# Merging the last gate products, the out-projection and the MLP of a transformer layer into one block

## The reference, cut to what matters

```python
    g_f, g_d, g_g, g_c = jnp.split(jax.nn.sigmoid(gate_logits), N_BRANCHES, axis=-1)
    merged = (g_f * (y_f @ lp['w_br_fourier']) + g_d * (o_d @ lp['w_br_diff'])
              + g_g * (o_g @ lp['w_br_gqa']) + g_c * (y_c @ lp['w_br_conv']))
    return merged @ lp['w_out']
...
# then, per stream, with rms norms and modulation:
x = x + gx1 * rms_norm(mixer_out); x = x + gx2 * rms_norm(sq_relu_mlp(modulate(x)))
```

## Time and profile before

| | us |
|---|---|
| median of 3 runs | 3958.98 |
| lowest, highest run | 3958.79, 3963.68 |
| span of the profiled execution (first to last instruction) | 3959.9 |
| PE busy in it | 3646.2 (92%) |
| DVE, ACT, POOL busy in it | 1911.9, 1398.4, 131.7 |
| mean granted PE clock, share of full speed | 0.953 |

### The profile page before, as it was taken

The page is one execution under the profiler, slowest core; times in us unless marked ns, Lnnn a source line. Parts: engine busy times, 40 slices in busy tenths (PEclk is TensorE's granted clock), DMA queues, the critical chain, the costliest instruction groups (busy, mean ns, idle before and its releaser), DMA issues. The chain is left out here.

```text
span 3959.9 us, 47862 instructions
## 1 busy us (share of the span) xinstructions
PE 3646.2 (92%) x18756; PEld 2836.1 (72%) x18756; DVE 1911.9 (48%) x2912; ACT 1398.4 (35%) x2388; POOL 131.7 (3%) x90
## 2 busy tenths in 40 slices
PE   6989898979999999998897999989998999989999
PEld 2878897855677778884773567778887776677767
DVE  0756565655544354441475654434443346433553
ACT  2454433224443322222423444332222435334342
POOL 0000000010000010001001000010001000000000
PEclk9999898999999989997998999989998999989999
DMA  8425453320112323326331112223332221222212
GB/s 312 149 91 155 123 165 129 100 70 28 47 60 69 107 64 93 94 91 266 123 92 36 43 49 64 85 71 95 96 96 87 67 65 51 70 89 66 60 45 94
DMA packets 97407, 371.75 MB, mean 94 GB/s; under 512 B 11184, under 2 KB 11440, under 8 KB 95280
## 3 DMA queue, kind: packets, MB, share of 16 engines
q1 hardware_dynamic: 97200, 368.82, 29.2%
HBM read 357.25 MB, written 11.53 MB: 93 GB/s over the span
## 5 line engine op out<-in xcount | busy, mean ns | idle before, releaser
L368 DVE TENSOR_TENSOR w_lo<-w_raw,w_hi 128x1024 fp32r<-128x1024 f32 x527 | 644.9, 1224 | 776.7 <-ACT w_hi L358 776.4
L382 PE MATMUL banks<-h_hi,w_hi 128*128 128x512 f32 (+2 forms) x2040 | 790.3, 387 | 28.2 <-DVE h_lo L1005 9.8
L384 PE MATMUL banks<-h_hi,w_lo 128*128 128x512 f32 (+2 forms) x2040 | 749.5, 367 | 0.0
L383 PE MATMUL banks<-h_lo,w_hi 128*128 128x512 f32 (+2 forms) x2040 | 749.3, 367 | 0.0
L358 ACT ACTIVATE w_hi<-w_raw 128x1024 fp32r<-128x1024 f32 x545 | 573.0, 1053 | 363.6 <-DMA w_raw<-in_stream 361.6
L382 PEld LDWEIGHTS banks<-h_hi,w_hi 128*128 128x128 f32 (+1 forms) x2040 | 391.1, 192 | 118.6 <-issue 35.5
L384 PEld LDWEIGHTS banks<-h_hi,w_lo 128*128 128x128 f32 (+1 forms) x2040 | 390.1, 191 | 66.4
L383 PEld LDWEIGHTS banks<-h_lo,w_hi 128*128 128x128 f32 (+1 forms) x2040 | 391.9, 192 | 56.6 <-issue 3.8
L382 PE MATMUL banks<-merged_hi,w_hi 128*128 128x512 f32 (+1 forms) x960 | 350.0, 365 | 28.1 <-PEq L2320 10.7
L384 PE MATMUL banks<-merged_hi,w_lo 128*128 128x512 f32 (+1 forms) x960 | 346.4, 361 | 0.0
L383 PE MATMUL banks<-merged_lo,w_hi 128*128 128x512 f32 (+1 forms) x960 | 345.6, 360 | 0.0
(11 more groups left out here) (322 smaller groups left out, 4988.6 us busy)
## 6 DMA issues: line engine op xcount, KB each, us to landing
w_raw<-in_stream SPq DMA_DIRECT2D x593, 512.0 KB, 3.6
w_whole<-in_stream SPq DMA_DIRECT2D x48, 512.0 KB, 8.9
x_kept<-x SPq DMA_DIRECT2D x4, 2048.0 KB, 7.2
x<-x_kept SPq DMA_DIRECT2D x4, 2048.0 KB, 8.1
dft_table<-in_dft SPq DMA_DIRECT2D x2, 2048.0 KB, 8.1
x<-in_x SPq DMA_DIRECT2D x1, 2048.0 KB, 11.2
out_x<-x SPq DMA_DIRECT2D x8, 256.0 KB, 4.4
late_consts<-in_consts SPq DMA_DIRECT2D x1, 1152.0 KB, 5.5
```

Source lines behind the costliest of these rows:

```text
L368: (by or self.nc.vector).tensor_tensor(self.lo[:, c], self.raw[:, c], self.hi[:, c].bitcast(F32), ALU.subtract)\
L382: self.nc.tensor.matmul(out, w_hi, x_hi, start=start, stop=False)
L383: self.nc.tensor.matmul(out, w_hi, x_lo, start=False, stop=False)
L384: mm = self.nc.tensor.matmul(out, w_lo, x_hi, start=False, stop=stop)
```

## The change

The function `merge_last_branch` goes. Its PE, ACT and DVE parts stand at the head of the parts of `rest_stage`, in the same block as the out-projection. PE's first out-projection tile waits, ahead of each k, for `merged_lo[k]`. The block of `begin_transfer` for `x` goes too: SP issues that DMA as its first instruction of the joined block, so ahead of the last gate products instead of behind them, and ahead of the weight loads of that block. POOL and DVE wait for it before the first residual, as they did. As the two blocks' buffers now live together, `y` is laid over `branch_sum`, `mid_hi` and `mid_lo` over `h`, the squares over the gate tiles; `x` is placed from the top of memory (`take_high`), and the three little tiles of the norm that outlives the function have fixed homes. No arithmetic is added or removed.

```diff
@@ -435,6 +435,19 @@
         self.held.append((at, at + size, t.name))
         return t
 
+    def take_high(self, name, shape, dt=F32):
+        size = -(-4 * int(np.prod(shape)) // 64) * 64
+        at = self.high - size
+        for a, b, _ in sorted(self.held, key=lambda h: -h[0]):
+            if b <= at:
+                break
+            at = min(at, a - size)
+        assert at >= self.low, (name, size)
+        self.n += 1
+        t = self.nc.alloc_sbuf_tensor_at(f"{name}_{self.n}", [P] + list(shape), dt, offset=at)
+        self.held.append((at, at + size, t.name))
+        return t
+
     def over(self, name, t, dt, shape=None, skip=0):
 
         self.n += 1
@@ -881,12 +894,13 @@
 
 
 
-    def __init__(self, K, name, n_tiles, NT, at, rows_bank):
+    def __init__(self, K, name, n_tiles, NT, at, rows_bank, home=None):
         self.K, self.n, self.NT, self.nt = K, n_tiles, NT, NT // P
         self.sums = K.ps[:, 7, at:at + n_tiles * self.nt]
         self.rows = K.ps[:, rows_bank, 0:NT]
         self.sq = None
-        self.mean, self.rt, self.rstd = (K.take(f"{name}_{t}", [self.nt]) for t in ("mean", "root", "rstd"))
+        self.own = [K.take(f"{name}_{t}", [self.nt]) for t in ("mean", "root", "rstd")] if home is None else []
+        self.mean, self.rt, self.rstd = [t[:] for t in self.own] or [home[:, j] for j in range(3)]
         S = lambda t: K.count_of(f"{name}_{t}")
         self.squared, self.summed, self.averaged = S("squared"), S("summed"), S("averaged")
         self.rooted, self.inverse, self.turned = S("rooted"), S("inverse"), S("turned")
...
@@ -1011,7 +1025,7 @@
             s.advance(self.n)
 
 
-def rest_stage(K, x, merged, mod, mods, NT, following):
+def rest_stage(K, x, merged, mod, mods, NT, following, gates, h, kept):
@@ -1022,15 +1036,16 @@
     scaled, added = S("rest_scaled"), (S("rest_added_dve"), S("rest_added_pool"))
     up_free, down_free, mid_hi_ready, mid_lo_ready = S("mlp_up_bank_free"), S("mlp_down_bank_free"), S("mlp_mid_hi"), S("mlp_mid_lo")
     h_hi, h_lo = merged
-    c0, up, turns = W.used, W.used + KD, FF_T // 8
-    per = 2 * CHUNK
-    x_in = [(count.sem, count.at(value)) for count, value, _ in K.owed]
+    gates.merged = merged
+    c0, turns = gates.ends.next_block // CHUNK, FF_T // 8
+    up, per = c0 + KD, 2 * CHUNK
+    x_in = K.count_of("x_in")
     with ExitStack() as scope, K.block() as block:
-        y = K.sb(scope, "y", [KD, NT])
-        mid_hi = K.sb(scope, "mid_hi", [8, NT], F32R)
-        mid_lo = K.sb(scope, "mid_lo", [8, NT], F32R)
+        y = K.over("y", gates.acc, F32)
+        mid_hi = K.over("mid_hi", h[0], F32R)
+        mid_lo = K.over("mid_lo", h[1], F32R)
         m = K.sb(scope, "mid", [2, NT])
-        sq = K.sb(scope, "squares", [4, NT])
+        sq = K.over("squares", gates.sg, F32)
         table = K.sb(scope, "table_load", [1])
         post_mix = RowNorm(K, "post_mix", KD, NT, 0, 4)
         pre_mlp = RowNorm(K, "pre_mlp", KD, NT, 32, 5)
@@ -1040,18 +1055,31 @@
                 norm.sq = sq
         lead = Lead(K, pre_mlp, x, mods[:, 2], mod[:, 24:32], h_hi, h_lo, NT, False)
         lead.t = m
+
+        @block.sync
+        def _(sp):
+            if kept is not None:
+                sp.dma_start(x[:].rearrange("p k n -> p (k n)"), kept).then_inc(x_in.sem, 16)
         run_pipeline_ahead(K, block, up + per * turns)
         K.settle(block)
 
+        def wait_x(eng):
+            if kept is not None:
+                eng.wait_ge(x_in.sem, x_in.at(16))
+
         def wait_added(eng, n):
             eng.wait_ge(added[n % 2].sem, added[n % 2].at(n // 2 + 1))
 
         @block.tensor
         def _(pe):
+            for _ in gates.pe(pe, 2):
+                pass
             for f in range(KD):
                 if f >= 4:
                     pe.wait_ge(post_mix.squared.sem, post_mix.squared.at(f - 3))
                 for k in range(KD):
+                    if f == 0:
+                        pe.wait_ge(gates.out_lo.sem, gates.out_lo.at(k + 1))
                     W.multiply(pe, K.ps[:, f % 4, 0:NT], (c0 + f) * CHUNK + k, h_hi[:, k, 0:NT], h_lo[:, k, 0:NT],
                                k == 0, k == KD - 1)
                 if f >= 1:
@@ -1092,6 +1120,8 @@
 
         @block.scalar
         def _(act):
+            for _ in gates.act(act, 2):
+                pass
             nc.scalar.activation(table[:], K.eps[:], ACT.Sqrt)
             for f in range(KD):
                 W.split_hi(act, c0 + f + AHEAD)
@@ -1130,8 +1160,7 @@
                     nc.gpsimd.tensor_tensor(x[:, f, 0:NT], x[:, f, 0:NT], m[:, f % 2], ALU.add).then_inc(added[1].sem, 1)
 
             lead.pool(pool, range(up + AHEAD, up + SLOTS))
-            for sem, value in x_in:
-                pool.wait_ge(sem, value)
+            wait_x(pool)
             residual(0)
             residual(KD)
@@ -1152,10 +1181,11 @@
                         nc.vector.tensor_tensor(x[:, f - 1, 0:NT], x[:, f - 1, 0:NT], m[:, (f - 1) % 2], ALU.add)\
                             .then_inc(added[0].sem, 1)
 
+            for _ in gates.dve(dve, 2):
+                pass
             for f in range(KD):
                 W.split_lo(dve, c0 + f + AHEAD)
-            for sem, value in x_in:
-                dve.wait_ge(sem, value)
+            wait_x(dve)
             residual(post_mix, mods[:, 1], 0)
             wait_added(dve, KD - 2)
             wait_added(dve, KD - 1)
@@ -1197,6 +1227,9 @@
     lead.close()
     for norm in (post_mix, pre_mlp, post_mlp):
         norm.close()
+    if kept is not None:
+        x_in.advance(16)
+    gates.close()
     W.used = up + per * turns
     K.give_settled()
@@ -1723,31 +1756,6 @@
     return gates, y_hi
 
 
-def merge_last_branch(K, gates, merged):
-
-
-    gates.merged = merged
-    with K.block() as block:
-        run_pipeline_ahead(K, block, gates.last_block(2) // CHUNK)
-
-        @block.tensor
-        def _(pe):
-            for _ in gates.pe(pe, 2):
-                pass
-
-        @block.scalar
-        def _(act):
-            for _ in gates.act(act, 2):
-                pass
-
-        @block.vector
-        def _(dve):
-            for _ in gates.dve(dve, 2):
-                pass
-    gates.close()
-
-
-
 def split_stage(K, items):
 
     nc = K.nc
@@ -2448,11 +2456,7 @@
     for s in sources:
         if s.done:
             s.give(K)
-    merged = (K.take("merged_hi", [KD, NT], F32R), K.take("merged_lo", [KD, NT], F32R))
-    merge_last_branch(K, gates, merged)
-    K.give(branch)
-    K.give(y_hi)
-    return merged
+    return gates, branch, y_hi
 
 
 def block_one_stream(K, x, vec, lam, mod, mods, NT, kv, sources, rope, dft, before=None, after=None, kept=None):
@@ -2462,15 +2466,13 @@
     lead = Lead(K, before or RowNorm(K, "pre_mix", KD, NT, 0, 5), x, mods[:, 0], mod[:, 0:8], h[0], h[1], NT, before is None)
     if kept is not None:
         begin_transfer(K, kept, x[:].rearrange("p k n -> p (k n)"), "x_out", x)
-    merged = mixer(K, lead, vec, lam, NT, kv, sources, rope, dft)
-    K.give(h[0])
-    K.give(h[1])
+    gates, branch, y_hi = mixer(K, lead, vec, lam, NT, kv, sources, rope, dft)
+    merged = (K.take("merged_hi", [KD, NT], F32R), K.take("merged_lo", [KD, NT], F32R))
     if kept is not None:
-        x = K.take("x", [KD, NT])
-        begin_transfer(K, x[:].rearrange("p k n -> p (k n)"), kept, "x_in")
-    rest_stage(K, x, merged, mod, mods, NT, after)
-    K.give(merged[0])
-    K.give(merged[1])
+        x = K.take_high("x", [KD, NT])
+    rest_stage(K, x, merged, mod, mods, NT, after, gates, h, kept)
+    for t in (branch, y_hi) + h + merged:
+        K.give(t)
     return x
@@ -3382,6 +3384,7 @@
         K = Core(nc, ctx, A["stream"])
         K.consts = K.take("consts", [N_EARLY])
         K.eps = K.take("eps", [1])
+        norm_homes = [K.take(f"norm_{n}", [3, SEQ // P]) for n in range(2)]
         x = K.take("x", [KD, SEQ])
         lam = K.take("lam", [2, 8])
         vec = K.take("vectors", [VEC1_N])
...
@@ -3445,7 +3448,7 @@
                 K.give(c)
             kv_x = KV(K, "latent", SEQ)
             kv_c.done = kv_x.done = True
-            before, after = after, RowNorm(K, "following", KD, SEQ, 96, 5)
+            before, after = after, RowNorm(K, "following", KD, SEQ, 96, 5, norm_homes[l])
             x = block_one_stream(K, x, vec, lam[:, l], mod[:, 0], mods[:, 0], SEQ, kv_x, [kv_x, kv_c], A["rope"],
                                  A["dft512"], before, after, x_kept)
         K.give(vec)
...
```

More of the change, by code:

```diff
@@ L908, in average @@
         dve.wait_ge(self.summed.sem, self.summed.at(self.n))
-        self.K.nc.vector.reduce_sum(self.mean[:], self.sums.rearrange("p (k i) -> p i k", i=self.nt), AX_X)\
+        self.K.nc.vector.reduce_sum(self.mean, self.sums.rearrange("p (k i) -> p i k", i=self.nt), AX_X)\
             .then_inc(self.averaged.sem, 1)
@@ L913, in root @@
         act.wait_ge(self.averaged.sem, self.averaged.at(1))
```

(8 more changed lines are left out.)

## The result

The changed kernel takes **3929.1 us** (median of 4 runs, 3928.5 to 3937.9) against 3961.3 of the kernel before in runs beside it: a ratio of 0.9925 with a 95% interval of 0.991 to 0.994, so about 30 us less, where 19 were forecast. The profiled execution has a span of 3927.6 us at a mean granted clock of 0.955; before it was 3959.9 at 0.953.

What follows compares the result with a forecast made beforehand. PE, busy 92% of the span, was taken to set the time, through its idle gaps and lower clock. Gains of 7.3 + 7.0 + 4.7 = 19.0 us, other terms 0, gave 3940.0 us from 3958.98; range 3937 to 3947.

Steps and rivals of the forecast that it cites:

- The idle gaps, latent: Last branch matmul to out-projection, latent layers 0 and 1: idle and half-clock matmuls go, 7.3 and 7.0 us gained.
- The context: Same boundary, context stream: PE still waits about 1.0 and 1.3 us for merged tiles 6 and 7; 4.7 us gained.
- rival B: The clock falls in the context's two short waits, costing 2 us, so the time is 3942; chance 0.10.
- The added waits: Eight semaphore waits in the first out-projection tile of each call: taken as 0, at most 1.7 us.
- ACT and DVE behind the gate products: Context, Sqrt table load ahead of the split for the third tile: nothing lost, 0.4 us to spare.
- The x transfer: x moved ahead of the weight loads: taken as 0, with 0 to 2.5 us kept for each latent call.
- The rival D: Out-projection held until all of merged is written, only passages between blocks go: 2.5 us, 3956.5; chance 0.05.
- The overlaid buffers add no wait of their own: 0: Memory, buffers laid over each other in the joined block: no added wait, 0 us.
- small shifts in the 3900 us behind: Work behind the boundaries: with a chain ending earlier than read, some 3 us downwards in the range.

Runs made afterwards that it cites:

- two tiles abreast: The changed kernel with the first two out-projection tiles computed together, both for each k behind the same wait: 3932.9 us, ratio 0.9922.
- one whole wait: The changed kernel with the first out-projection tile waiting once, ahead of k = 0, for all eight merged tiles: 3955.1 us, ratio 0.9981.
- the aligned pair: The kernel before and the changed kernel, each with every tile of 4 KB or more placed at 128 within 256 bytes: 3940.4 and 3917.1 us.

## Why the prediction was wrong in size and right in kind

- **The idle gaps, latent:** 7.3 and 7.0 forecast, 7.28 and 7.02 measured. No wait is left there and the clock stays at 1.00. Right.
- **The context:** 4.7 forecast for the second tile's start, 4.39 measured, then 1.1 lost at the lower clock. That is rival B, to which I gave 0.10. At the third tile the context is 1.4 us short of the forecast, 1.1 of it by the lower clock, where B said 2. What spoke against it was full clock behind one idle of 1.55 us. Behind two, of 0.81 and 1.08 us, with 0.6 us of work between them, the clock fell. With two tiles abreast one idle of 0.82 us in the same place left the clock at 1.00. The Trainium skill (TensorE: Matmul & The Clock Gate, A second HAM failure mode: psum-queue depth-cycling) tells of a kernel whose frequent short idles between groups of matmuls made the clock go up and down; the trace agrees with that.
- **The added waits:** 0 forecast. In the latent calls no idle time stands at any of them. Right.
- **ACT and DVE behind the gate products:** in the changed kernel PE does not wait at the third tile in the context, so the table load was covered. Right. With two tiles abreast PE did not wait for that split either, but for the second tile's.
- **The x transfer:** 0 forecast, 0 within what a comparison can tell. The two transfers that were moved landed in 8.9 and 9.5 us instead of 7.7 and 9.1; the split due meanwhile in layer 0 was on time, and PE waits for nothing there.
- **The rival D:** I priced the passages alone at 2.5 us; one whole wait left 0.5 us, and 3.6 in the aligned pair. The reading was right, that the waits tile by tile carry the join.
- **The step that failed** is the one on memory: "The overlaid buffers add no wait of their own: 0", and beside it the "some 3 us" downwards for "small shifts in the 3900 us behind". No wait was added, and that is where I stopped. The homes and overlays moved the operands of nearly all later matmuls against the weights modulo 256, and PE's own rhythm with them, from 232.4 to 228.9 ns in the gate products. Where the forecast had 0, the homes alone gave 12 us in the kernel before (8 to 17), and moving the operands back by 64 bytes cost the changed kernel 17 to 22. With it the sum comes out: 17.6 at the joins and 12 from the homes are 29.6, and the ratio says 30 (24 to 36). That the two agree so closely is in part luck: in the traces the distances alone explain 7.4 of the 12 and 5.6 of the 15, and the clock in the two stretches above makes up most of the rest. Whether that clock hangs on the offsets too stays open. The trace of before holds a sign of it, had I looked: its gate products stand 232.4 ns apart and its second out-projection 229.6, with no idle time in either.

## What to carry to other kernels

A change that allocates, frees or overlays buffers is never only what its instructions say: before costing it at nothing, list where each matmul operand lands, modulo 256 against the weights, before and after, the hi and the lo part each. When a gain is larger than the sum, line the two traces up matmul by matmul; what comes in proportion to work, at a full clock and with no idle time, is the rhythm of the engine and not a wait. Joining two blocks pays through the waits that it lets one split: the consumer must wait piece by piece, or the join gives almost nothing.

## What the runs showed of the hardware that I had not expected

- The distance between fp32r matmuls (three per product, 512 columns) depends on the place of the moving operand against the weights modulo 256 bytes: 226.9, 228.9, 232.3 and 233.3 ns at 0, 64, 128 and 192, with the hi and the lo part at the same place. That is 2.8% between best and worst, at full clock and with nothing else running. With 256 columns the order is another: 119.9 ns at 0, 117.8 at 64.
- With the two parts at different places it is 228.8 to 233.4 ns by another rule, which these runs don't give: hi at the weights' own place and lo 128 bytes off can be slower (233.4) than both 128 off (232.3).
- At one and the same address there can be a second value: 228.9 or 233.3 ns for a whole stage of 150 us, another one in another execution of the same program. What picks it stays open.
- Behind two idles of 0.81 and 1.08 us, 0.6 us of work apart, the clock was down (0.57), where one of 1.55 us and one of 0.82 us had left it up.
